# A diffusion layer with an expert mixer: each expert-row gather waits until at most two issued row sets are still on the way

## The reference

```python
def chunk_fn(hc):                       # 128 tokens at a time
    q = (hc @ wq).reshape(PEER_CHUNK, PEER_HEADS, 2, D_HALF)
    s = jnp.einsum('chsd,hskd->chsk', q, subkeys)
    vals, idx = lax.top_k(s, PEER_TOPK)
    ...
    g = jax.nn.softmax(sc.astype(jnp.float32), axis=-1).astype(hc.dtype)
    act = jax.nn.gelu(jnp.einsum('chkd,cd->chk', u[ex], hc), approximate=False)
    return jnp.einsum('chk,chkd->cd', g * act, v[ex])
```

## Time and profile before

| What | us |
|---|---|
| Median of 3 runs | 2161.32 |
| Lowest and highest run | 2153.51, 2171.27 |
| Span of the profiled execution | 2140.9 |
| Busy in it: PE, DVE | 1739.1, 1291.6 |
| Busy in it: ACT, POOL | 620.4, 1171.9 |

### The profile page before, as it was taken

The page is one execution under the profiler, slowest core; times in us unless marked ns, Lnnn a source line. Parts: engine busy times, 40 slices in busy tenths (PEclk is TensorE's granted clock), DMA queues, the critical chain, the costliest instruction groups (busy, mean ns, idle before and its releaser), DMA issues.

```text
span 2140.9 us, 25754 instructions
## 1 busy us (share of the span) xinstructions
PE 1739.1 (81%) x8614; PEld 875.4 (41%) x8614; DVE 1291.6 (60%) x3250; ACT 620.4 (29%) x1497; POOL 1171.9 (55%) x1555
## 2 busy tenths in 40 slices
PE   6998999988888868789879887667767777676776
PEld 3544445777756323344434432223223222232232
DVE  1289863777656956555565655647556565655543
ACT  3256512454542313122222222112212212221111
POOL 2100014556535666666666666666666666666664
PEclk8999999999999998999999998889898889898899
DMA  7466464545399898999999999999999999999997
GB/s 246 130 201 219 161 186 123 149 109 149 64 328 339 295 377 334 362 390 391 379 391 383 383 369 371 378 358 391 358 382 364 364 371 377 372 371 363 378 369 298
DMA packets 282156, 659.70 MB, mean 308 GB/s; under 512 B 71248, under 2 KB 120496, under 8 KB 282032
## 3 DMA queue, kind: packets, MB, share of 16 engines
q0 software_dynamic: 150336, 552.67, 67.7%
q1 hardware_dynamic: 131696, 105.46, 16.5%
HBM read 635.49 MB, written 22.54 MB: 307 GB/s over the span
## 4 chain that ended last, share of the span: by engine, by line
PE 31%; issue 13%; POOL 13%; DMA 7%; another core or an unknown queue 5%; DVE 2%; ACT 2%; ACTq 1%; POOLq 0%; DVEq 0%
PE banks L2113 23%; POOL arena L1662 12%; DMA arena<-in_peer_v_dram,arena 5%; PE banks L2134 4%; PE banks L564 1%; PE banks L1561 1%; DMA arena<-in_peer_u_dram,arena 1%; DVE arena L2063 1%; ACTq L1369 1%; PE banks L2142 0%; ACT arena L1716 0%; PE banks L1142 0%; ACT L1813 0%; ACT L1738 0%
## 5 line engine op out<-in xcount | busy, mean ns | idle before, releaser
L2113 PE MATMUL banks<-arena 128*128 128x512 f32 x1984 | 985.9, 647 | 298.8 <-issue 243.6
L2063 DVE CUSTOM_DVE_ANT_0 arena<-arena,banks 128x1024 f32<-128x1024 f32 x503 | 612.0, 1218 | 386.0 <-DMA arena<-in_peer_u_dram,arena 322.7
L2113 PEld LDWEIGHTS banks<-arena 128*128 128x128 f32 x1984 | 390.9, 205 | 879.2 <-issue 836.5
L1662 POOL DMA_INDIRECT arena<-in_peer_v_dram,arena x504 | 479.2, 951 | 336.3 <-remote 128.4
L1662 POOL DMA_INDIRECT arena<-in_peer_u_dram,arena x512 | 484.3, 946 | 174.1 <-issue 149.8
L1716 ACT ACTIVATE arena<-arena 128x128 f32<-128x128 f32 x496 | 182.0, 397 | 858.6 <-remote 360.5
L1142 PE MATMUL banks<-arena 64*64 64x64 f32 (+1 forms) x2688 | 108.8, 231 | 14.8 <-POOL arena L796 7.0
L2744 PE MATMUL banks<-arena 128*128 128x512 f32 x224 | 110.9, 602 | 0.7 <-ACT arena L2389 0.7
L1142 PEld LDWEIGHTS banks<-arena 64*64 64x64 f32 x2688 | 95.9, 136 | 29.8 <-issue 12.2
L2134 PE MATMUL banks<-arena 128*128 128x384 f32 x256 | 85.8, 486 | 0.0
L2840 PE MATMUL banks<-arena 128*128 128x512 f32 x192 | 84.8, 597 | 0.4 <-issue 0.4
(11 more groups left out here) (365 smaller groups left out, 2001.5 us busy)
## 6 DMA issues: line engine op xcount, KB each, us to landing
arena<-in_w_mod_dram SPq DMA_DIRECT2D x18, 1024.0 KB, 7.4
arena<-in_peer_wq_dram SPq DMA_DIRECT2D x16, 1024.0 KB, 6.7
arena<-in_w_in_dram SPq DMA_DIRECT2D x27, 512.0 KB, 8.0
arena<-in_peer_u_dram,arena POOLq DMA_INDIRECT x512
arena<-in_peer_v_dram,arena POOLq DMA_INDIRECT x512
arena<-in_w_mod_dram SPq DMA_DIRECT2D x3, 2048.0 KB, 11.6
bk_scratch<-arena POOLq DMA_DIRECT2D x8, 768.0 KB, 4.9
kr_scratch<-arena POOLq DMA_DIRECT2D x8, 768.0 KB, 6.7
```

The source lines that it names most:

```text
L1662: pool.indirect_dma_start(ring[:, j % RING, :], None, table, bass.IndirectOffsetOnAxis(ap=idx[:, hi % 4, j:j + 1].bitcast(U32), axis=0)).t ...
L2063: nc.vector.tensor_tensor_reduce(u_ring[:, j % RING, :], u_ring[:, j % RING, :], h2_row, 1.0, 0.0, ALU.mult, ALU.add, acts[:, h % 2, j:j + ...
L2113: m = nc.tensor.matmul(PO[h][:, :], diag[:, j % 4], v_ring[:, j % RING, 512 * h:512 * h + 512], start=hp == 0 and j == 0, stop=hp == HEADS ...
```

## The change

`pool6` keeps a list of the sets that `gather` has issued, each with its semaphore and the value that this has once the set has landed. From the fourth call on, `gather` waits for the set issued three calls before. At the moment of an issue at most two sets of `gather` are therefore on the way, three after it. The wait for the ring slot stays in front of it. The calls in `tail` that don't go through `gather` neither wait nor count.

```diff
@@ -1616,6 +1616,7 @@
     NSL = TOPK
     FROM_SBUF = 3
     V_LAG = 4
+    IN_FLIGHT = 3
@@ -1654,11 +1655,16 @@
     def pool6(pool):
+        issued = []
+
         def gather(kind, g, hi, j, first):
 
             ring, table, sems, used = [(u_ring, peer_u[0], u_rows, dots), (v_ring, peer_v[0], v_rows, experts_added)][kind]
             if not (first and hi == 0 and j < RING):
                 pool.wait_ge(used, NSL * g + j + 1 - RING)
+            if len(issued) >= IN_FLIGHT:
+                pool.wait_ge(*issued[-IN_FLIGHT])
+            issued.append((sems[j % RING], 32 * g + 16 * (j // RING) + 16))
             pool.indirect_dma_start(ring[:, j % RING, :], None, table,
                                     bass.IndirectOffsetOnAxis(ap=idx[:, hi % 4, j:j + 1].bitcast(U32), axis=0)
                                     ).then_inc(sems[j % RING], 16)
```

## The result

The changed kernel takes 2699.32 us (median of 4, 2698.29 to 2699.38), the kernel before in the same comparison 2161.56 us (4 runs, 2153.51 to 2171.27). The ratio is **1.2505, 95% interval 1.2457 to 1.2552**: slower by 538 us, where +307 was forecast and the range ended at 2600.

The account below looks back on a forecast made before the run. The prediction took the DMA engines as the limit within bursts, with GpSimd's pauses letting them run dry. 1008 x 1.727 = 1741, plus 25, less 1458.7 gave +307 us on 2161, so 2468 us, range 2250 to 2600.

Parts of the forecast that it names:

- the DMA engines are the limit within bursts: Expert stage before the change: a row set costs the DMA engines 1.28 us, against 1.24 us per gather issued.
- A limit of two outstanding binds at nearly every gather: Bursts of gathers: 7.19 us from issue to use at 1.24 us per issue means some five other sets queued.
- A satisfied wait costs 0: Added wait before 1013 gathers: executing it already satisfied was taken as 0, at most 0.30 us a gather.
- The cycle at a shallow queue: Gather start to landing plus GpSimd's waking: 5.18 us taken, a third of it giving a period of 1.73 us.
- DVE's waking in it stands for GpSimd's: Within the 5.18 us cycle: VectorE's waking was taken to cover GpSimd's, with no separate term.
- the upper end of 5.6 us: Longest cycle allowed, called halfway between 5.18 and 6.15 us; it gives a period of 1.87 us.
- The 25 us of extras: Added to the stage: remaining early waits for chosen experts and 16 query-weight loads of 1 MB, 25 us.
- The 20.4 us between span and median: Whole run: the difference between the 2140.9 us span and the 2161.3 us median was taken to stay.
- Rival 1: Expert stage: spaced sets land sooner, cycle 4.4 to 4.8 us, period 1.45 to 1.60, 2190 to 2340 us; chance 0.25.
- Rival 2: Expert stage: the limit costs nothing and the pauses go, not slower, 1992 to 2161 us; chance 0.05.
- rival 3: TensorE becomes the bound, its clock staying at 1.2 GHz, 3.78 us a row, 2642 us; chance 0.07.
- Rival 4: Added waits do less than said: landings already seen late or waits mostly satisfied, 2161 us; chance 0.03.

Follow-up runs that it names:

- e7: Kernel before, no limit, each gather fetching 2 KB per partition instead of 4 KB and dot products taking 512 columns; 2156.0 us, ratio 0.999.
- e3: Changed kernel with five row sets in flight instead of three; 2171.39 us, ratio 1.006 to the kernel before.
- e4: Changed kernel with eight row sets in flight instead of three; 2165.57 us, ratio 1.0024 to the kernel before.
- e1: Changed kernel with the two waits swapped in the source, so the gather carries the landing wait; 2589.98 us, ratio 1.199 to the kernel before.
- e11: Changed kernel with two row sets in flight instead of three; 3338.42 us, ratio 1.5556 to the kernel before.
- e2: Changed kernel with four row sets in flight instead of three; 2366.54 us, ratio 1.0974 to the kernel before.
- e18: Kernel before with half the bytes per gather, eight diagonals instead of four, and the first 512 columns of 14 of 16 products omitted; 2139.58 us, ratio 0.9913.

## Why the prediction was right in direction and wrong in size

**What bounded the kernel before.** The pauses, the bursts of 1.24 us and the queue of some five sets were read rightly, but "the DMA engines are the limit within bursts" was not shown: at half the bytes (e7) the stage takes the same time. This did no harm, since the new period is above both.

**A limit of two outstanding binds at nearly every gather.** Right: a landing held 929 of 1024. At five sets in flight (e3) it holds 180, which fits the five others read from the 7.19 us.

**A satisfied wait costs 0.** Right by e4.

**The cycle at a shallow queue: the step that failed.** It had two parts. The first, from issue to a user's start, was taken as 5.18 us and measured 5.21. The second was one clause, "DVE's waking in it stands for GpSimd's". It doesn't: GpSimd starts 0.74 us after VectorE for the same landing. That is 0.74 / 3 = 0.247 us a period, x 1008 = **249 us**. The forecast added 307 us to the span, with it 556; the span grew by 556.5. That the two agree to a microsecond is in part luck, since small terms on both sides were not measured apart. The restart was not bounded at all: the upper end of 5.6 us allowed for a deeper queue and nothing for GpSimd (and halfway between 5.18 and 6.15 is 5.67, not 5.6). I had seen that a gather at a head boundary has two waits, costed the second only for the case where it is satisfied, and didn't ask what it costs when it is the one that ends last. e1 shows that the order of the waits sets 0.50 of the 0.76 us.

The trace of before had the price in it. Two u gathers there wait for the same kind of event, the end of a dot product, which frees their slot. These are the ends of the two dots on VectorE:

```profile
717.01 0.08 DVE L2063 DVE_READ_ACCUMULATOR2_ANT arena<- 128x1 f32 x1
...
720.68 0.08 DVE L2063 DVE_READ_ACCUMULATOR2_ANT arena<- 128x1 f32 x1
```

and these the gathers that they release:

```profile
717.37 0.94 POOL L1662 DMA_INDIRECT arena<-in_peer_u_dram,arena  x1 [0.47 <-DVE arena L2063]
...
721.54 0.94 POOL L1662 DMA_INDIRECT arena<-in_peer_u_dram,arena  x1 [1.99 <-DVE arena L2063]
```

The first carries its only wait and starts 0.28 us after the dot's end (717.09). The second stands at a head boundary, where the slot's wait is written second and so is one of the 32 that stand alone:

```profile
L1661 POOLq EVENT_SEMAPHORE  x32: 17/17/17, 654.0 to 2041.3; - x32
```

It starts 0.78 us after the dot's end (720.76). With such a restart of 0.74 us more than VectorE's the forecast would have been 2468 + 249 = 2717 us, inside 1% of the 2699.

**The 25 us of extras.** The mean cycle of 6.00 us is 0.03 above the median of a u set; the sum closes with these 25 us in it, and they weren't measured apart.

**The 20.4 us between span and median, "taken to stay".** They didn't: after, the span is 2697.4 of 2699.38. The profiled execution of before was a quick one among its runs. This makes the 556 us of the span 538 of the medians.

**TensorE and the rings.** PE kept up, at 1140 us in L2119 instead of 986 because more of its work ran at the lower clock, 1.2 GHz: 426 of the 1984 matmuls took over 800 ns, where 204 did before; it stayed under the 1400 us that I had named. ACT's unexplained waits went, as forecast, and gave nothing back beside the longer period. DMA share 0.82 lies in the forecast 0.75 to 0.85; 269 GB/s is below the 300 to 320, in the ratio of the periods. The tail kept its pace:

```profile
2676.09 1.02 POOL L1711 DMA_INDIRECT arena<-in_peer_v_dram,arena  x1 [0.30 <-issue]
2677.41 0.93 POOL L1668 DMA_INDIRECT arena<-in_peer_v_dram,arena  x1 [0.30 <-issue]
2678.64 1.02 POOL L1711 DMA_INDIRECT arena<-in_peer_v_dram,arena  x1 [0.30 <-issue]
```

**The rivals.** Rival 1, that spaced sets land sooner, fell: at 2.0 us between issues a set still takes 5.21 us with two ahead of it. One ahead instead (e11) gives 4.37 us, three (e2) 5.77 us, so the sets ahead count most. The spacing counts for less: at the same depth and 1.89 instead of 2.00 us between issues (e1) it is 5.30 us. Its lowest period, for a cycle of 4.4 us, is 1.47 and not 1.45. Rival 2 fell; the shortest median from issue to use of a whole row set, in e11, is 4.37 us. The estimate of 3.2 us for a row set, worked out from the fit in the Trainium skill ("DMA: Bandwidth & Descriptors", section "Anatomy of one DMA — SWDGE (gpsimd) path"), is below every one of these medians; a set with none ahead of it was not run. In rival 3 the direction of the clock was right and its effect nil. Rival 4 fell.

**Where the range went wrong.** Its upper end was 2600 us, by a cycle of 5.6 us. A cost for the restart of GpSimd between 0 and one more issue gap of 0.30 us would have given 5.9 us and, with the 25 us, 1008 x 5.9 / 3 + 25 - 1458.7 = 549 us, an upper end of 2710 us. That holds the measured 2699, but only because its two parts are off in opposite ways: the restart is 0.74 us and not 0.30, and the allowance of 0.42 us for a deeper queue was hardly needed (0.03). The gather at 721.54 in the trace of before would have given the value itself.

## What to carry to other kernels

If an issue is tied to an earlier landing, the period is (issue to landing + restart of the issuing engine) / transfers in flight. Take the restart from that engine, not from a consumer, and from a row where the same kind of wait ends last. Where two waits stand before one instruction, look in the trace which of them it carries and which stands alone (EVENT_SEMAPHORE, with its own line), and arrange that it carries the one that will end last. In these kernels it carries the one that the source writes first, which is not the one that stands nearest to it in the source. A full DMA share doesn't show that bytes are the bound: halve them once before believing it. A limit on depth is free only where it no longer binds: with eight row sets here no cost shows, with five it is 0.6%.

## What the runs showed of the hardware that I had not expected

- **A wait that stands alone costs more than one that is carried.** GpSimd's gather starts 0.74 us after VectorE (0.63 after TensorE) when the landing wait is an instruction of its own ahead of it, and 0.24 (0.12) us when the gather carries that wait. From the last count of the landing it is 0.76 and 0.26 us.
- **Landing time grows with depth.** From issue to use 4.37, 5.21 and 5.77 us with one, two and three sets ahead, where 0.524 MB take 1.28 us of the DMA engines. Half the bytes, with two sets ahead, took it from 5.21 to 3.61 us.
- **The stage runs at one gather of 128 rows per 1.44 to 1.47 us**, with 2 KB or 4 KB a row, DMA share 0.65 to 0.99, and bursts of 1.24 to 1.35 us. Near that rate the counts of TensorE come up to 10.8 us late by the trace and in clusters, and VectorE waits for its own for up to 7.7 us (e18). At 1.54 us a gather and slower none was late.
- The store of 768 KB from GpSimd's queue landed in 3.6 us instead of 4.9 in the changed kernel, with nothing in that stage changed; over all the runs it is 3.6 to 4.9. Such a row scatters by a third, and I had used it as a lower bound.
